# A two-block transformer forward pass on one core: where the causal attention's head pairs are multiplied with the values

## The reference, cut to what matters

```python
p = rmsnorm(x, g) @ w_in              # q, k, v and gate are column ranges of p
s = q @ k.T * scale + bias            # causal or windowed mask in the bias
pr = softmax(s)                       # swa: with a sink in max and denominator
y = (pr @ v) * silu(gate)
x = x + y @ w_out
```

## Time and profile before

| | us |
|---|---|
| median of 3 executions | 1764.2 |
| their range | 1763.42 to 1774.3 |
| the profiled execution, its own time | 1765.29 |
| the profiled execution, span from first to last instruction | 1763.5 |
| busy TensorE (matmul) | 1741.1 |
| busy VectorE | 1309.9 |
| busy ScalarE | 900.3 |
| mean granted TensorE clock | 0.998 |

### The profile page before, as it was taken

How to read it: one execution, slowest core, us unless ns; L and a number is a source line. 1 busy time by engine, 2 the same in 40 slices (tenths; PEclk the granted TensorE clock), 3 DMA queues, 4 the chain that set the end, 5 groups by cost and what they waited for, 6 DMA issues and landing times.

```text
span 1763.5 us, 35702 instructions
## 1 busy us (share of the span) xinstructions
PE 1741.1 (99%) x14357; PEld 1665.8 (94%) x14357; DVE 1309.9 (74%) x2085; ACT 900.3 (51%) x1326; POOL 41.4 (2%) x48
## 2 busy tenths in 40 slices
PE   8999999999999999999999999999999999999997
PEld 8999999999999999999999899998989999999876
DVE  7899889986779987998776765556555666677754
ACT  5433664545544355546465464545454553666553
POOL 0000000000000000000000110000100000000000
PEclk9999999999999999999999999999999999999999
DMA  7576645565656665556566656665755556555553
GB/s 234 181 214 198 191 145 167 187 199 197 202 179 206 196 198 150 154 186 209 182 198 191 199 185 203 190 190 167 210 159 180 192 180 190 159 159 178 168 190 131
DMA packets 200082, 326.07 MB, mean 185 GB/s; under 512 B 14911, under 2 KB 66319, under 8 KB 199821
## 3 DMA queue, kind: packets, MB, share of 16 engines
q1 hardware_dynamic: 197085, 320.58, 58.3%
q10 hardware_dynamic: 2864, 3.62, 0.7%
HBM read 320.42 MB, written 2.69 MB: 183 GB/s over the span
## 4 chain that ended last, share of the span: by engine, by line
PE 83%; DVE 13%; ACT 1%; issue 1%; DMA 1%; ACTq 0%; DVEq 0%; POOLq 0%; SPq 0%; POOL 0%
PE g L501 64%; PE g L512 11%; DVE w_lo L912 6%; DVE cacc L1158 5%; PE att L609 2%; PE att L655 2%; PE att L633 2%; ACT w_hi L1547 1%; DVE glu L1130 0%; DVE glu L1121 0%; PE att L803 0%; ACTq L1535 0%; DMA turned<-q 0%; DMA stage<-in_w_in_dram 0%; DVE gate L1121 0%
## 5 line engine op out<-in xcount | busy, mean ns | idle before, releaser
L912 DVE TENSOR_TENSOR w_lo<-stage,w_hi 128x1024 fp32r<-128x1024 f32 x577 | 706.5, 1233 | 367.9 <-ACT w_hi L1547 367.1
L1547 ACT CAST w_hi<-stage 128x1024 fp32r<-128x1024 f32 x577 | 598.9, 1050 | 603.7 <-PE g L501 393.7
L501 PE MATMUL g<-a_hi,w_hi 128*128 128x256 f32 x2496 | 702.1, 281 | 2.9 <-DVE w_lo L912 2.0
L501 PE MATMUL g<-a_lo,w_hi 128*128 128x256 f32 x2496 | 692.1, 277 | 0.0
L501 PE MATMUL g<-a_hi,w_lo 128*128 128x256 f32 x2496 | 692.1, 277 | 0.0
L501 PEld LDWEIGHTS g<-a_hi,w_hi 128*128 128x128 f32 x2496 | 470.3, 188 | 17.7 <-issue 14.3
L501 PEld LDWEIGHTS g<-a_hi,w_lo 128*128 128x128 f32 x2496 | 470.2, 188 | 0.5 <-issue 0.2
L501 PEld LDWEIGHTS g<-a_lo,w_hi 128*128 128x128 f32 x2496 | 470.1, 188 | 0.0
L501 PE MATMUL g<-b_hi,w_hi 128*128 128x256 f32 x1440 | 401.8, 279 | 1.5 <-DVE w_lo L912 1.4
L501 PE MATMUL g<-b_lo,w_hi 128*128 128x256 f32 x1440 | 398.6, 277 | 0.0
L501 PE MATMUL g<-b_hi,w_lo 128*128 128x256 f32 x1440 | 398.6, 277 | 0.0
(11 more groups left out here) (232 smaller groups left out, 1361.7 us busy)
## 6 DMA issues: line engine op xcount, KB each, us to landing
stage<-in_fox_w_in_dram SPq DMA_DIRECT2D x128, 512.0 KB, 4.1
stage<-in_w_in_dram SPq DMA_DIRECT2D x112, 512.0 KB, 3.8
stage<-in_swa_w_in_dram SPq DMA_DIRECT2D x72, 512.0 KB, 4.0
stage<-in_w_in_dram SPq DMA_DIRECT2D x128, 256.0 KB, 3.1
stage<-in_w_out_dram SPq DMA_DIRECT2D x64, 512.0 KB, 4.3
stage<-in_w_pg_dram SPq DMA_DIRECT2D x64, 512.0 KB, 4.2
stage<-in_fox_w_out_dram SPq DMA_DIRECT2D x32, 512.0 KB, 4.5
stage<-in_swa_w_out_dram SPq DMA_DIRECT2D x32, 512.0 KB, 3.8
```

The source lines that it names most:

```text
L501: mm = pe.matmul(acc[:, j * S:(j + 1) * S], w[:, slot, c0 + j * P:c0 + (j + 1) * P], xx[:, k, :], start=st and m == 0 and j % 2 == 0, stop ...
L912: dve.tensor_tensor(w_lo[:, slot, :], stage[:, slot, :], w_hi[:, slot, :].bitcast(F32), ALU.subtract).then_inc(*t.inc("w_split"))
L1547: act.copy(w_hi[:, slot, :], stage[:, slot, :]).then_inc(*t.inc("w_rounded"))
```

## The change

In the causal attention, pairs 0, 1 and 2 were one lot in slot 14 and pair 3 another in slot 15. Now pairs 0 and 1 are a lot in slot 12, between the transposes of pair 2 (slot 11) and those of pair 3 (slot 13); pairs 2 and 3 are the other in slot 15. The fox wait `taken` moves with the first lot. The wait for copies is rewritten for the new place: at slot 12 three pairs have been turned, and all but the last two copies must be done. The attention of the first block (kind "full") keeps its one lot of four pairs, and its wait has the same value.

```diff
-                    pe.wait_ge(*t.again("t_free", GH - 2 - 2 * lot[-1]))
+                    pe.wait_ge(*t.again("t_free", 2 if lot[-1] == 1 else 0))
...
                 if kind == "full":
                     work[at + GH] = [attend(kind, values, range(GH // 2))]
                 else:
-                    work[at + GH - 1] = [*extra, attend(kind, values, (0, 1, 2))]
-                    work[at + GH] = [attend(kind, values, (3,))]
+                    work[at + GH - 3] = [*extra, attend(kind, values, (0, 1))]
+                    work[at + GH] = [attend(kind, values, (2, 3))]
```

## The result

The changed kernel takes 1786.3 us (median of 4 runs, 1782.28 to 1786.91) against 1768.65 us before (4 runs, 1763.42 to 1774.3): ratio 1.0094, 95% interval 1.0052 to 1.0137. The forecast was 1764.9 us in a range of 1762.2 to 1768.4. The change makes the kernel slower, by under 2% but by more than any of the rivals gave, and the prediction was wrong. The profiled execution took 1786.72 us.

The account below looks back on a forecast made before the run. TensorE's work in its written order was taken to bound the kernel. 0 for the work plus 0.7 us for the second half of the scores, on the 1764.2 us median, gave 1764.9 us, range 1762.2 to 1768.4.

Parts of the forecast that it names:

- the rivals: Slack takes all 1764.2 us (0.20); lots' size 1764.1 to 1767.3 (0.10); full delay 1768.4 (0.08); earlier end 1759.0 (0.04); nothing 1764.2 (0.03).
- The part on TensorE: Lots in each causal attention: 3.36 us removed, 3.36 us added, difference 0; bounds -0.8 to +2.4 us in all.
- Order: TensorE's written order: changing it matters only if moved work costs another time or a covered chain makes TensorE wait.
- The sign of being wrong that I had named: TensorE waiting for copies or weights in the lots' chunk, or a projection-to-lot step differing from before.
- What is moved: Behind slot 12's lot: pair 3's transposes, copies and silu 1.68 us later, MB's gate product and swa's q 0.5 us later.
- The 0.7 us at the scores: Second half of swa scores, turns 2 to 4: q's 0.5 us delay exceeds the cover, costing 0.45 + 0.15 + 0.09 us.
- The covers: Slack before TensorE waits: 3.9 us for copies at slot 12, 2.2 at slot 15, 6.9 for weights; cost 0.
- The rule of the Trainium skill: ScalarE and VectorE take their queues strictly in order, so silu can't slip ahead of late copies; keeps the 0.7 us.
- The scatter: Whole-kernel runs: one of three lies 10 us above the others, so about 1% (18 us) can be told from no change.

Follow-up runs that it names:

- three behind: Kernel before with causal transposes one slot earlier and three lots behind them (slots 13, 14, 15); median 12 us over before.
- fox only: Kernel before with the change's new lots in the four fox attentions alone, swa as before; ratio to before 1.0027, fox stretch 507.5 us (+9.7).
- one lot: Kernel before with all four pairs of a causal attention in one lot in slot 15; median 8.1 us over before.
- two at the end: Kernel before with pairs 0 and 1 in slot 14, pairs 2 and 3 in slot 15; ratio to before 0.9996.

## Why the prediction was wrong

- **The part on TensorE: the step that failed.** "The difference is 0, because the number of lots, of pairs and of changes between projection and attention stays the same." The terms were right: a lot of two pairs takes 1.45 us, as interpolated. What failed is the term for the projection behind a lot. I took 0.23 us, over 12 matmuls, for all of it. That is only the change from one kind of work to the other, and it is paid at either pace: 12 matmuls behind a lot take 1.61 us when they are slow and 1.58 when they are fast ("three behind"). The pace which a lot leaves was no term of the sum. The slow pace goes on until the next insert: 1.68 us over 384 matmuls in each of three fox turns (45.42 - 43.74), 3.4 us over the 774 behind the last. In each of the three turns 90 more steps of the next attention, up to its first transposes, are slow too (0.4 us). That adds up to 9.7 us, the figure of "fox only"; the change has 9.5, as a stretch of 48 matmuls at the start of swa is fast in it and slow before. The earlier trace rows could hardly show this: of its 0.23 us the slow steps are about 0.05 (11 steps at 4.5 ns).
- **Order.** I held that the order matters only by another cost of the moved work or by a covered chain. There is a third way: what the moved work leaves behind for the unmoved. The transposes between the two lots decided it. The sign of being wrong that I had named, another step from the projection to the lot, did not show: that step is 206 to 209 ns in both profiles. The steps far behind the lot are the ones that differ.
- **What is moved** was right. The first swa turn of the changed kernel on ScalarE and VectorE, to be read against the earlier trace rows:

```profile
1542.90 0.86 ACT L1612 COPY u<-att 128x384 f32<-128x384 f32 x2 [3.31 <-PE att L633]
...
1546.02 1.06 ACT L1556 ACTIVATE gate<-gate 128x1024 f32<-128x1024 f32 x1
```

```profile
1547.27 1.28 DVE L1047 TENSOR_TENSOR gate<-gate,att 128x512 f32<-128x512 f32 x2 [1.31 <-ACT gate L1556]
```

  The copies waited 3.31 us for TensorE, 1.7 us more than the 1.59 before; silu ended at 1547.08, and the two products with OB and MB ran one behind the other. The last lot ended at 1547.38, so MB's product was about 0.5 us late, as worked out.
- **The 0.7 us at the scores** did not come. TensorE's list has no wait for L1006 at all. In the second turn the read ends at 1569.78 and the scores start at 1570.27. The issue of the swapping DMAs did come 0.4 us later behind the last lot, near the 0.5 us worked out. But the projection ahead of the first scores runs at the slow pace now (17.16 and not 16.54 us for 144 matmuls), which puts the scores 0.6 us later. The projection between the halves went the other way, from the slow pace to the fast, and takes back 0.15 us of it; these rows are before and after:

```profile
1546.45 4.44 PE g L501 x36
```

```profile
1566.05 4.29 PE g L501 x36
```

  The second half of the scores thus starts 0.47 us later behind the last lot than before, and the reads end only 0.1 to 0.5 us later. What the late q would have cost at before's pace no run shows. The last read and the scores behind it, after:

```profile
1569.70 0.08 DVE L1006 DVE_READ_ACCUMULATOR2_ANT mx<- 128x1 f32 x1
```

```profile
1570.27 1.58 PE L609 MATMUL att<-kk,q 64*128 64x128 f32 x16
```

- **The covers** of copies, weights and gates held; from 980 us on the list has no wait for any (those for split weights, L912, lie in the first block).
- **The rule of the Trainium skill** on the order of the queue ("TensorE: Matmul & The Clock Gate", the section on the array of 32×32 sub-arrays) held as far as the trace shows: the silu, at 1546.02, did go back with the copies. It had no say in the result.
- **The scatter.** I saw runs of before at 1764 and 1774 and took about 10 us for noise of the measurement. By their distances, and by kernels whose profile had the slow stretches and most of whose other runs were 8 to 12 us shorter ("one lot", "two at the end"), it is the same two paces, in two stretches of the first block. 11.6 to 12.5 us of the profiles' 21.4 are the change (two profiles of it have the same fox and swa times within 0.1 us), the rest is chance. With 4 runs each the first comparison had this chance in it too; 22 and 6 runs gave 1.0065 (1.0044 to 1.0087).

## What to carry to other kernels

When TensorE never waits and the count of its instructions is fixed, still compare the time of long equal stretches (so many matmuls in so many us, from the chain that ended last) and not only lists of waits. Check an insert's cost over the whole stretch behind it, up to the next insert, and not by the first dozen instructions. Where runs of one kernel fall into groups a few us apart, look for the stretch that changes between executions before taking the distance for noise.

## What the runs showed of the hardware

- Dense projection matmuls (float32r, 128x128 weights, 256 columns) run at one of two steady paces, 113.3 or 117.8 ns a step, at an unchanged granted clock. Both last over 1000 matmuls.
- A group of products whose outputs take 64 partitions each, in 8 to 32 records, turned the pace in 241 of 241 cases. Score groups (64 rows of weights), reached without a wait, turned it in 253 of 254.
- Six 128x128 transposes kept the fast pace in 261 of 261 cases without a wait and turned the slow one in 58 of 96; with a wait ahead they left the slow one in all 7 cases. Eight in a row, in the first block, turned the fast pace into the slow one in 52 of 56 cases.
- A near-wait in front of an insert (a step of 219 to 227 ns to `spread_rs`, where 118 is usual) goes with a pace behind it that differs between profiles with the same code there, for 4.7 us in a stretch of 1068 matmuls.
- Why TensorE has two paces, and what in an insert turns them, no run here shows.
